# The gated delta recurrence: inverse by 32x32 tiles and a four-chunk pipeline written out

## The reference

```python
def step(S, blk):
    qc, kc, vc, gc, bc = blk
    G = jnp.cumsum(gc, axis=-1)
    diff = G[..., :, None] - G[..., None, :]
    decay = jnp.where(incl, jnp.exp(jnp.where(incl, diff, 0.0)), 0.0)
    kk = jnp.einsum('bhtd,bhid->bhti', kc, kc)
    A = jnp.where(strict, bc[..., :, None] * decay * kk, 0.0)
    eG = jnp.exp(G)
    rhs = bc[..., None] * (vc - eG[..., None] * jnp.einsum('bhtd,bhde->bhte', kc, S))
    U = lax.linalg.triangular_solve(A + eye, rhs, left_side=True, lower=True, unit_diagonal=True)
    qk = jnp.einsum('bhtd,bhid->bhti', qc, kc) * decay
    o = eG[..., None] * jnp.einsum('bhtd,bhde->bhte', qc, S) + jnp.einsum('bhti,bhie->bhte', qk, U)
    w_end = jnp.exp(G[..., -1:] - G)
    S_new = eG[..., -1, None, None] * S + jnp.einsum('bhid,bhie->bhde', kc * w_end[..., None], U)
    return S_new, o
```

## Time and profile before

| | us |
|---|---|
| median of 3 executions (lowest, highest) | 3022.9 (3021.7, 3024.1) |
| the profiled execution, its own time | 3023.9 |
| its span | 3022.1 |
| TensorE busy | 2854.6 (94%) |
| VectorE busy | 1542.6 (51%) |
| ScalarE busy | 962.2 (32%) |
| GpSimd busy | 583.8 (19%) |

### The profile page before, as it was taken

The page is one execution under the profiler, slowest core; times in us unless marked ns, Lnnn a source line. Parts: engine busy times, 40 slices in busy tenths (PEclk is TensorE's granted clock), DMA queues, the critical chain, the costliest instruction groups (busy, mean ns, idle before and its releaser), DMA issues. The chain is left out here.

```text
span 3022.1 us, 45985 instructions
## 1 busy us (share of the span) xinstructions
PE 2854.6 (94%) x18498; PEld 2741.4 (91%) x18498; DVE 1542.6 (51%) x2304; ACT 962.2 (32%) x1691; POOL 583.8 (19%) x321
## 2 busy tenths in 40 slices
PE   6999988979999999999989999996899999999997
PEld 5999978859999999999979888884899999999996
DVE  4057434346753444443482577774676434444436
ACT  3325534425411111111152456663451111111113
POOL 1212134400122222222200121210003222222210
PEclk8999989979999999999999999997999999999999
DMA  4111100033321111111141221214332111111103
GB/s 146 51 43 36 30 10 0 1 91 107 108 71 55 42 42 42 42 42 51 32 134 31 66 90 59 90 56 152 119 108 70 43 55 42 42 42 42 42 14 114
DMA packets 183492, 184.96 MB, mean 61 GB/s; under 512 B 10469, under 2 KB 168549, under 8 KB 183296
## 3 DMA queue, kind: packets, MB, share of 16 engines
q1 hardware_dynamic: 183380, 183.45, 19.3%
HBM read 151.13 MB, written 32.57 MB: 61 GB/s over the span
## 5 line engine op out<-in xcount | busy, mean ns | idle before, releaser
L1560 DVE TENSOR_TENSOR acc<-acc,ps 128x1032 f32<-128x1032 f32 x144 | 177.0, 1229 | 231.9 <-PE ps L124 231.9
L1964 PE MATMUL ps<-mix_in0hi,in0wh 128*128 128x344 f32 x600 | 197.1, 329 | 13.1 <-POOL mix_in0lo L247 7.9
L124 PE MATMUL ps<-midlo,rest0wh 128*128 128x344 f32 x984 | 209.1, 321 | 0.0
L124 PE MATMUL ps<-mix_out1lo,rest1wh 128*128 128x344 f32 x984 | 209.0, 321 | 0.0
L124 PE MATMUL ps<-midhi,rest0wl 128*128 128x344 f32 x984 | 208.6, 320 | 0.0
L124 PE MATMUL ps<-mix_out1hi,rest1wh 128*128 128x344 f32 x984 | 208.6, 320 | 0.0
L124 PE MATMUL ps<-midhi,rest0wh 128*128 128x344 f32 x984 | 208.5, 320 | 0.0
L124 PE MATMUL ps<-mix_out1hi,rest1wl 128*128 128x344 f32 x984 | 208.5, 320 | 0.0
L1964 PE MATMUL ps<-mix_in0lo,in0wh 128*128 128x344 f32 x600 | 192.5, 321 | 0.0
L1964 PE MATMUL ps<-mix_in0hi,in0wl 128*128 128x344 f32 x600 | 192.4, 321 | 0.0
L124 PEld LDWEIGHTS ps<-midhi,rest0wl 128*128 128x128 f32 x984 | 165.6, 188 | 0.0
(11 more groups left out here) (508 smaller groups left out, 6917.4 us busy)
## 6 DMA issues: line engine op xcount, KB each, us to landing
wraw<-in_w_ffn_gate SPq DMA_DIRECT2D x22, 1024.0 KB, 5.3
wraw<-in_w_ffn_up SPq DMA_DIRECT2D x22, 1024.0 KB, 5.3
wraw<-in_w_ffn_down SPq DMA_DIRECT2D x22, 1024.0 KB
wraw<-x_scratch SPq DMA_DIRECT2D x96, 172.0 KB, 3.0
x_scratch<-acc SPq DMA_DIRECT2D x72, 172.0 KB, 2.9
wraw<-in_w_in_even SPq DMA_DIRECT2D x24, 512.0 KB, 3.8
wraw<-in_w_in_odd SPq DMA_DIRECT2D x24, 512.0 KB, 4.6
sr_page<-in_cache_k SPq DMA_DIRECT2D x16, 512.0 KB, 4.1
```

Source lines behind the costliest of these rows:

```text
L124: ins = pe.matmul(ps[:, 3 * r + c, 0:CH], w, h[:, c * CH:(c + 1) * CH], start=first and n == 0, stop=last and n == 2)
L1560: dve.tensor_tensor(a, a, region(T.ps, m % 2), ALU.add).then_inc(collected, 1)
L1964: ins = pe.matmul(bank(n, c), w[n % 2][:, k, :], cut(h[:, k, :], c), start=first and m == 0, stop=final and m == 2)
```

## The change

Only `stage_delta` changes; its inputs and outputs are the same. The seven levels of 128x128 become:

- Five small levels (blocks of 1, 2, 4, 8, 16 rows) inside the four 32x32 blocks on the diagonal. They lie compactly, 128 partitions x 32 columns a head (`lc`, `am`, `tc`, `ttc`). Products run on 32x32 tiles of the array, one for each block, at tile positions (32j, 32j). VectorE turns the blocks with its 32x32 transpose instead of TensorE. GpSimd masks all five levels with one instruction.
- A merge of 32 rows (`off_32`, `merge_32`) and one of 64 rows (`off_64`, `merge_64`) then fill `tt`, the full transposed inverse.

The staging copies are gone: the program of every engine is written out for all chunks, so matmuls read `qkv` and `gates` in place. Keys are turned once, moved by ScalarE, and scaled by GpSimd, which also scales values and queries, in place in `qkv`. The spread uses 32 rows of the array where it used 64. One round of the pipeline holds four chunks: f = r + 3 (scores), y = r + 2 (small levels), z = r + 1 (merges of 32 and 64, keys), r (recurrence); r goes from -3 to 7, eleven rounds. The state has two buffers, and its update waits only for the outer product. The constants come by nine DMAs.

The diff, cut to its core; of the new functions the lines of the new side stand (the removed ones are in the kernel printed above), and lines of only "..." mark what is left out:

```diff
@@ -2233,312 +2233,473 @@
...
-    LV = 7
-    UP = LV - 1
+    B = 32
+    SMALL = 5
+    NB = P // B
+    heads = range(H)
...
-        am = T.wraw[:].rearrange("p (x l h n) -> p x l h n", x=2, l=LV - 1, h=H)
...
+        masks, sel, cap, ident = sb("masks", [P, SMALL, B]), sb("sel", [64, 8, P]), sb("cap", [P, P]), sb("ident", [P, B])
+        col, eg_col, beg, wend = (sb(n, [P, 3, w]) for n, w in (("col", 64), ("eg_col", H), ("beg", H), ("wend", H)))
+        eg_end = sb("eg_end", [P, NCHUNK, H])
+        eg, dm, tt, w2, u, state = (sb(n, [P, 2, H, P]) for n in "eg dm tt w2 u state".split())
+        lt, kbe = (sb(n, [P, 3, H, P]) for n in "lt kbe".split())
+        pt = sb("pt", [P, 4, H, P])
+        lc, am = sb("lc", [P, H, B]), sb("am", [P, 2, SMALL, H, B])
+        tc, ttc = sb("tc", [P, 3, H, B]), sb("ttc", [P, 3, H, B])
+        p1, p5 = sb("p1", [P, H, B]), sb("p5", [P, H, B])
+        ta, p6 = sb("ta", [P, H, 2 * B]), sb("p6", [P, H, 2 * B])
+        bank = [T.ps[:, n, :].rearrange("p (h n) -> p h n", h=H) for n in range(8)]
+        small = [T.ps[:, n, 0:H * B].rearrange("p (h n) -> p h n", h=H) for n in range(8)]
+        wide = T.ps[:, 6, 0:H * 2 * B].rearrange("p (h n) -> p h n", h=H)
+        cols = lambda c: slice(P * c, P * c + P)
+        Q = lambda c, h: qkv[:, h, cols(c)]
+        K = lambda c, h: qkv[:, H + h, cols(c)]
+        V = lambda c, h: qkv[:, 2 * H + h, cols(c)]
+        rows = lambda j, n=1: slice(B * j, B * (j + n))
...
+                for j in range(NB):
+                    level = consts[rows(j), C_LEVEL:C_LEVEL + SMALL * P].rearrange("p (l n) -> p l n", l=SMALL)
+                    sp.dma_start(masks[rows(j)], level[:, :, rows(j)]).then_inc(con_in, 16)
+                    sp.dma_start(ident[rows(j)], consts[rows(j), C_ID + B * j:C_ID + B * j + B]).then_inc(con_in, 16)
...
+                dve.memset(state[:, 0], 0.0)
+                dve.memset(tt[:], 0.0)
+                dve.memset(ta[:], 0.0)
...
+                def spread_gates(c):
...
+                            r = slice(32 * half, 32 * half + 32)
+                            pe.matmul(bank[1 - half][:, h, :], sel[r, H * half + h, :], gates[r, cols(c)],
+                                      start=True, stop=True)
...
+                def off_block(c, l):
+                    pe.wait_ge(updated, SMALL * c + l)
+                    pe.wait_ge(masked, c + 1)
                     for h in heads:
+                        for j in range(NB):
+                            ins = pe.matmul(small[4][rows(j), h, :], am[rows(j), c % 2, l, h, :], tc[rows(j), c % 3, h, :],
+                                            start=True, stop=True, tile_position=(B * j, B * j))
+                    ins.then_inc(p1_made, 1)
+                def merge(c, l):
+                    pe.wait_ge(p1_moved, (SMALL - 1) * c + l)
+                    pe.wait_ge(turned, SMALL * c + l)
                     for h in heads:
+                        for j in range(NB):
+                            ins = pe.matmul(small[5][rows(j), h, :], ttc[rows(j), c % 3, h, :], p1[rows(j), h, :],
+                                            start=True, stop=True, tile_position=(B * j, B * j))
+                    ins.then_inc(merged, 1)
+                def off_32(c):
+                    pe.wait_ge(updated, SMALL * c + SMALL)
+                    if c:
+                        pe.wait_ge(tt_done, c)
                     for h in heads:
+                        for j in (0, 2):
+                            ins = pe.matmul(small[6][rows(j + 1), h, :], lt[rows(j), c % 3, h, rows(j + 1)],
+                                            tc[rows(j), c % 3, h, :], start=True, stop=True, tile_position=(B * j, B * j + B))
+                    ins.then_inc(p5_made, 1)
+                def merge_32(c):
+                    pe.wait_ge(p5_moved, c + 1)
+                    pe.wait_ge(turned, SMALL * c + SMALL)
                     for h in heads:
+                        for j in (0, 2):
+                            pe.matmul(small[6][rows(j), h, :], p5[rows(j + 1), h, :], ttc[rows(j + 1), c % 3, h, :],
+                                      start=True, stop=True, tile_position=(B * j + B, B * j))
+                        ins = pe.matmul(small[6][rows(1), h, :], ttc[rows(1), c % 3, h, :], p5[rows(1), h, :],
+                                        start=True, stop=True, tile_position=(B, B))
+                    ins.then_inc(r5_made, 1)
+                def off_64(c):
+                    pe.wait_ge(r5_moved, c + 1)
                     for h in heads:
+                        ins = pe.matmul(wide[rows(2, 2), h, :], lt[rows(0, 2), c % 3, h, rows(2, 2)], ta[rows(0, 2), h, :],
+                                        start=True, stop=True, tile_position=(0, 2 * B))
+                    ins.then_inc(p6_made, 1)
+                def merge_64(c):
+                    pe.wait_ge(p6_moved, c + 1)
                     for h in heads:
+                        ins = pe.matmul(wide[rows(0, 2), h, :], p6[rows(2, 2), h, :], tt[rows(2, 2), c % 2, h, rows(2, 2)],
+                                        start=True, stop=True, tile_position=(2 * B, 0))
+                    ins.then_inc(r6_made, 1)
...
+                for r in range(-3, NCHUNK):
+                    z, y, f = r + 1, r + 2, r + 3
+                    has_r, has_z, has_y, has_f = (0 <= c < NCHUNK for c in (r, z, y, f))
+                    if has_f:
+                        spread_gates(f)
+                    if has_y:
+                        off_block(y, 1)
+                    if has_z:
+                        off_32(z)
+                    if has_r:
+                        solve(r)
+                    if has_y:
+                        merge(y, 1)
+                    if has_f:
+                        key_key(f)
+                    if has_z:
+                        merge_32(z)
+                    if has_y:
+                        off_block(y, 2)
+                    if has_r:
+                        outer(r)
+                    if has_y:
+                        merge(y, 2)
+                    if has_z:
+                        off_64(z)
+                    if has_f:
+                        key_query(f)
+                    if has_y:
+                        off_block(y, 3)
+                    if has_r:
+                        output(r, heads[0:2])
+                    if has_y:
+                        merge(y, 3)
+                    if has_z:
+                        merge_64(z)
+                    if has_r:
+                        output(r, heads[2:4])
+                    if has_y:
+                        off_block(y, 4)
+                    if has_f:
+                        turn_keys(f)
+                    if has_y:
+                        merge(y, 4)
+                    if has_z:
+                        keys(z)
+                    if has_f:
+                        turn_values(f)
...
+                def first(c):
+                    dve.wait_ge(masked, c + 1)
+                    dve.tensor_tensor(ttc[:, c % 3], over(ident[:], H), am[:, c % 2, 0], ALU.subtract).then_inc(turned, 1)
+                    dve.wait_ge(turned, SMALL * c + 1)
+                    dve.transpose(tc[:, c % 3].rearrange("p h n -> p (h n)"), ttc[:, c % 3].rearrange("p h n -> p (h n)")
+                                  ).then_inc(updated, 1)
+                def update(c, l):
+                    dve.wait_ge(merged, (SMALL - 1) * c + l)
+                    dve.wait_ge(updated, SMALL * c + l)
+                    dve.tensor_tensor(tc[:, c % 3], tc[:, c % 3], small[5], ALU.subtract).then_inc(updated, 1)
+                    dve.wait_ge(updated, SMALL * c + l + 1)
+                    dve.transpose(ttc[:, c % 3].rearrange("p h n -> p (h n)"), tc[:, c % 3].rearrange("p h n -> p (h n)")
+                                  ).then_inc(turned, 1)
+                def place(c):
+                    x = c % 2
+                    dve.wait_ge(turned, SMALL * c + SMALL)
+                    for j in range(NB):
+                        dve.tensor_copy(tt[rows(j), x, :, rows(j)], ttc[rows(j), c % 3])
+                    for j in range(2):
+                        dve.tensor_copy(ta[rows(j), :, rows(j)], tc[rows(j), c % 3])
+                def take_32(c):
+                    x = c % 2
+                    dve.wait_ge(r5_made, c + 1)
+                    for j in (0, 2):
+                        dve.tensor_scalar(tt[rows(j), x, :, rows(j + 1)], small[6][rows(j)], -1.0, None, ALU.mult)
+                    dve.tensor_scalar(ta[rows(1), :, rows(0)], small[6][rows(1)], -1.0, None, ALU.mult).then_inc(r5_moved, 1)
+                def take_64(c):
+                    dve.wait_ge(r6_made, c + 1)
+                    dve.tensor_scalar(tt[rows(0, 2), c % 2, :, rows(2, 2)], wide[rows(0, 2)], -1.0, None, ALU.mult
+                                      ).then_inc(tt_done, 1)
...
+                def new_state(c):
+                    x = c % 2
```

(60 more changed lines are left out.)

394 lines of the change are left out of this document (170 added, 224 removed).

## The result

The changed kernel takes 2969.1 us (median of four runs, 2964.4 to 2971.5) where the kernel before takes 3022.6 (now the median of four; the first three had 3022.9): a ratio of 0.982, with a 95% interval of 0.980 to 0.984. The forecast was 2970. The profiled run took 2970.2, its span is 2968.4.

What follows compares the result with a forecast made beforehand. The prediction took TensorE to bound the kernel. Five full rounds (106.5 us), filling and draining (78.5) and a later start (about 1.5) gave 186.5 us for the stage's 239.1, hence 2970 us, range 2936 to 3010.

Steps and rivals of the forecast that it cites:

- Price of a tile record: Recurrence, TensorE: 0.0255 us for each 32x32 tile record, 296 a chunk, 7.5 us, or 8.4 with the merge of 64.
- Spread: Spreading the gates on TensorE: 16 records at 0.117 us, 1.9 us a chunk, with no side-by-side running of halves counted on.
- rival 4: More is gained in the round: spread tiles pair, shape changes hide, no low clock; round 17.5 us, 2941 us; chance 0.15.
- Changes of shape: TensorE's round alternates full matrices with tiles: 20 changes at 0.09 to 0.10 us each, 2.0 us a round.
- No other engine ends later: In the round, the level chain and tail, 15 us, stay under TensorE's round; VectorE's sum is 11.6 us.
- Clock: TensorE in the round: some rounds have a stretch at 1.2 GHz after small work, 0.9 us a round.
- Round: One full pipeline round: 10.0 + 8.4 + 2.0 + 0.9 = 21.3 us.
- Filling and draining: Pipeline's ends: three filling rounds of 11, 18 and 18 us; draining of 16, 9.5 and 6 us.
- What follows the stage is unchanged: Stages behind the recurrence: taken at the same time as before, so no gain or loss there.
- (1): Recurrence tiles run one after another, sharing one PSUM bank: 34 us more, 3004 us; chance 0.15.
- (2): Tile matmuls don't bring or hold TensorE's 2.4 GHz, so the kernel ends slower; 3037 us at half; chance 0.10.
- (3): Late hand-overs hold up TensorE's in-order stream of four chunks: 3.5 us a round, 28 more, 2998 us; chance 0.08.

Runs made afterwards that it cites:

- 12: As 11, but five small matmuls instead of one at each of the four places: 2960.5 us, round 18.07 us.
- 11: On top of version 2, one small matmul at each of four places, eight more changes of the array's shape a round: 2948.7 us, round 17.06 us.
- version 2: The changed kernel with the six placements made by ScalarE and no longer by VectorE: 2934.4 us, round 15.6 us.
- experiment 3: The changed kernel with GpSimd's three scalings cut to 4 columns instead of 512, outputs wrong: 2934.5 us, round 15.7 us.
- 1: The changed kernel with the next chunk's first inverse ahead of the six placements on VectorE: 2947.6 us, round 17.0 us.
- 8: The changed kernel with 40 one-column ScalarE copies, read by nothing, ahead of the stage: 2965.0 us.
- experiment 4: The changed kernel with the two loops of the four tile levels exchanged, so heads of one tile follow each other: 3000.6 us.
- version 7: On top of version 2, selectors loaded first, before the stage's barrier, with masks and identity behind it: 2930.9 us.
- 9: On top of version 7, matmuls that nothing reads where TensorE would idle in the filling and the draining: 2920.8 us.

## Why the prediction was right, and where its steps were off

The total was right and the mechanism of the gain too: tiles side by side, a round with TensorE's work cut, four chunks to hide the chain. That the total comes so near is luck, since errors of either sign cancel. Step by step:

- *Price of a tile record.* Taken 0.0255 from a row with four column groups; it is 0.0084. One tile alone costs 0.032 to 0.034 (12), so four side by side are a quarter of that. The row it was taken from has 128 weight rows and 128 moving columns; the step scaled the number of tiles and not the columns. Tile work is 296 x 0.0084 + 1.0 = 3.5 us a round, not 8.4. **The largest error, 4.9 us a round.**
- *Spread.* The pairing of its halves, put into rival 4, happens: 0.95 us and not 1.9.
- *Changes of shape.* 20 x 0.1 was taken; 11 gives 0.147 each, 2.9 us. With that, 9.05 + 3.5 + 2.9 = 15.5 us, and the round of version 2, which TensorE fills, is 15.6. These terms account for all but 0.2 us.
- *"No other engine ends later."* **This step failed.** Six placements were taken at 0.22 us, 1.2 in all, and the tail behind the last merge at 2.8 us beside 3.4 of cover. The sizes are right without GpSimd (0.218, experiment 3). Beside its scalings four placements take 4.03 us, and TensorE waits 3.1. The warning stood in the rows the text used: the earlier trace rows has VectorE at nearly twice its time (1257 ns against 691) for 512 columns in SBUF beside GpSimd, and it was weighed for the transpose alone, never for the copies, which fall where GpSimd starts.
- *Clock.* Taken 0.9 us a round from the chain of small work; it is 1.7 (half of 3.4), and its cause is the wait above: where the wait is gone or cut to pieces of at most 0.63 us (1, 2, 3), no full round after the first shows the low clock.
- *Round.* 15.6 + 3.1 + 1.7 = 20.4, measured 20.4, forecast 21.3. The errors cancel: tiles and spread were 5.8 us too dear, and the wait, the clock and the changes of shape 4.8 too cheap.
- *Filling and draining.* Forecast 47 and 31.5 us; measured 42.1 (389.1 to 431.2) and 34.9 (528.5 to the last output's move at 563.4). The first full round had no wait yet: the four placements ahead of it took 1.98 us, since GpSimd paused beside them. The five full rounds took 97.3 (15.7 and four of 20.4) where 106.5 were forecast. Start: 1.5 us taken, 0.4 measured. From the first spread that is 174.3 us for 185, and with the start 64.4 less than the 239.1 before, where 52.6 were forecast. (The 65.6 above also have 1.2 us less between the last move and the next stage.)
- *"What follows the stage is unchanged."* **Wrong by 10.2 us**: 2.0 in the sample-state stage, where TensorE has the low clock for longer (mean 0.59 for 0.60), and 8.0 in the attention stage. There the stretch with no engine at work has 4.2 and the 6.8 us at half clock behind it 3.4; why the engines stop stays open (8 speaks for late instructions). So the stage gained some 12 us more than forecast, and the rest of the kernel took 11.9 of it back (1.7 ahead, 10.2 behind).
- *Rivals.* (1) Row tiles held apart by their common bank: refuted. All four write one bank, each its own 32 partitions, and still run side by side; experiment 4 shows what the kernel would be without that, 3000.6 us, near the 3004 worked out. The rule of the Trainium skill cited there ("TensorEngine Tiling (Array Packing)", Gotcha 1: PSUM Pressure) has no effect on time in this trace (0.0084 us a record). (2) Small tiles don't bring or hold the clock: refuted for the full rounds, those of version 2 run at 2.4 GHz throughout. Whether they bring it is open: in the filling of version 7 the clock was at 1.2 GHz for 27.3 us (395.7 to 423.0), with TensorE busy for 25.2 of them. The text's sign, a clock above 0.9 in the stage, wasn't met: it was 0.87, by the filling (0.66). (3) A late hand-over, 3.5 us a round: this is what happened in kind and size (3.1 us, with 1.7 for the clock), and its sign came, a wait with a name; the text gave it 0.08 and named no engine. Its time, 2998, didn't come, since the tiles were cheaper. (4) More gained: its condition holds for the spread and not for the changes of shape. Its time, 2941, lies between versions 1 and 2 (2947.6 and 2934.4), where (3) is partly or wholly taken away, but not by its sum, which has the tiles at 0.0255.

The best version (9) takes 2920.8 us, 48 us less than the changed kernel and 102 less than before.

## What to carry to other kernels

Check what GpSimd does at the time of each small copy of VectorE: a copy inside SBUF next to GpSimd's work took 4.6 times as long here (0.997 us for 0.218), ending only when GpSimd's instruction had ended, and moving six of them a chunk to ScalarE took another 26 us off a stage from which the whole change had taken 66. Issue small matmuls so that neighbours in the stream lie on different tiles of the array, and count every change of the tile's shape. When a stage's gain is judged, look at the stages behind it too, for the clock and for stops with no releaser.

## What the runs showed of the hardware

- Four 32x32 float tiles on the diagonal of the array, in one PSUM bank: 0.0084 us a record; one tile: 0.032 to 0.034; the loops exchanged: (0.89 - 0.19) / 31 = 0.023.
- A change of the tile's shape costs 0.147 us, measured with eight more a round.
- VectorE's copy of 32x128 floats inside SBUF: 0.218 us, beside GpSimd 0.997, ending 0.07 to 0.09 us behind one of GpSimd's instructions. A move of 64x256 out of PSUM: 0.42 us, beside GpSimd or not. The transpose of 32x32 blocks, 128x128 floats: 0.31 us, beside GpSimd or not. ScalarE's copy of 32x128: 0.307 us, beside GpSimd or not.
- After a wait of 3.1 us TensorE's clock was at 1.2 GHz for 3.4 us in every round; with the wait gone it stayed at 2.4. In the filling of version 7 it stayed low for 27 us, with TensorE busy for 25.2 of them.
- VectorE stopped for 4.6 and ScalarE for 5.2 us with no releaser, in a stretch where the DMA engines are 96% busy; forty more instructions of ScalarE ahead took ScalarE's stop away and left VectorE's (4.64 us).
